# Scaling of the gate one-hots moved from VectorE to ScalarE, eight row requests moved, and a separate buffer for the first gates

## The chip, the cores and the metric

The kernel runs on one core of a Trainium2 chip. The metric is the device time of one execution in microseconds (us). The engines are PE (TensorE, matrix multiply; PEld is its weight load), DVE (VectorE), ACT (ScalarE), POOL (GpSimd) and SP (SyncE, which here only issues DMAs). Each engine works through its own list of instructions in order, and the lists meet only at semaphores.

## The reference, cut to what matters

A two-block network over 512 tokens of width 1024. The change touches the expert layer of the first block. Each token picks 16 of 16,384 experts for each of 8 heads and mixes them with softmax gates:

```python
def peer_ffn(h, wq, sub_keys, u, v):       # D = 1024, 8 heads, top 16
    q = (t @ wq).reshape(PEER_BLOCK, PEER_HEADS, 2, PEER_DQ // 2)
    s = jnp.einsum('tpcd,pckd->tpck', q, sub_keys)
    s1, i1 = lax.top_k(s[:, :, 0], 16); s2, i2 = lax.top_k(s[:, :, 1], 16)
    ...
    top, pos = lax.top_k(cand, 16)         # cand: all s1 + s2; idx = i1 * 128 + i2
    g = jax.nn.softmax(top, axis=-1)
    a = jax.nn.gelu(jnp.einsum('tpkd,td->tpk', u[idx], t), approximate=False)
    return jnp.einsum('tpk,tpkd->td', (g * a), v[idx])
```

## The kernel before, in words

The expert layer is `phase_peer`. It treats the tokens in two ways. For 384 tokens (`DENSE`) it computes all 16,384 experts densely: `gelu(u @ h)` for every expert, times a gate matrix that is zero where an expert wasn't picked, times `v`. For the last 128 tokens it fetches the picked rows of `u` and of `v` from HBM by indirect DMA (`rows_by_index`, issued by POOL, 128 rows of 4 KB a request) and works on them on DVE (`dot`, `row`). Five row buffers (`RING`) are used in turn, so request n waits until row n - 5 was used.

The order of the work is written out by hand in steps g. Steps 0 to 3 are the output projection of the mixer, 4 to 11 the query projection, 12 to 75 the 64 groups of two 128-expert tiles of `u` (steps 12 to 75, "dense steps" below). In a dense step PE does two tiles j = 0, 1 of 24 matmuls each: every fp32 operand is split into a high and a low part (`split3`, lines 997 to 999). The high part `u_high` of step g is made by ACT (`high`, L1300), which may write it only when PE has ended step g - 2. The low part `u_low` is a subtraction, on POOL up to step 43 (L1182) and on DVE from step 44 (`low_u`, L1487). PE waits for it (`u_split`) at the start of the step. ACT also moves each finished tile out of PSUM through Gelu (L1353), into one of four tiles that SP stores (`spill`, L1112).

**Selection, steps 6 to 43.** PE makes scores in 16 units at the steps given by `unit_step` (14, 16, 18, 20, 23, ... 38 for the last twelve), and DVE finds the top 16 of each (`select`). Unit 4 (step 14) is followed by `row_numbers`, which gives the indices for the row requests (`indexed`). From step `PICK_AT` = 16 on, POOL issues the row requests of a step (`pick_step`) and then the subtraction of that step. DVE's products with these rows (`dot`, L1482) come at `dot_step`, ahead of the step's unit. At step 43 PE transposes the selection into `selT`.

**Spread, steps 44 to 67.** The gates are spread to dense form by a matmul of two one-hot matrices for each token. A batch m is 8 tokens, two batches a step: batch 2(g - 44) ahead of tile j = 0 and the next ahead of tile j = 1. DVE builds them (`batch`): one instruction for the eight `one2` (L1496) and eight for `one1`, each compare and multiply by the token's gate (L1499). PE multiplies them (`spread`, L1220), ACT moves the result to `gs` (L1344), and SP stores a block of 32 tokens every two steps.

**Steps 68 to 75** are dense steps with row requests and their products only. After them DVE does the last products, ACT a Gelu over all of them, and the second half begins: 64 groups `down(g)` with `v` (matmuls again at L997 to L999). For each, DVE multiplies the stored Gelu tile by the gates (`weighted`, L1546), ACT makes `v_high` (L1361) and `w_high` (L1365), DVE `v_low` (L1537) and `w_low` (L1553), and then some row sums (`row`, L1530 and L1533). Three of these row sums (`rows_at[0]`) stand between `w_low` of group 0 and the work for group 1; the second of them reads its row into the buffer of `h_tok`, which is free only when all 128 products are done.

Of the kernel before, what the change touches and what calls it, by code (L numbers as in the profile page):

```python
# [16 lines left out]
ALU = mybir.AluOpType  # L17
# [130 lines left out]
def phase_project(k):  # L148
    nc, ps = k.nc, k.ps
    with ExitStack() as ctx:  # L150
# [32 lines left out]
        rows_in, rows = k.sem("c_rows_loaded"), k.sem("c_rows_ready")  # L183
# [100 lines left out]
        def _(dve):  # L284
# [42 lines left out]
            dve.tensor_tensor(c_row[:], c_row[:], row_gate, ALU.mult).then_inc(rows, 1)  # L327
            dve.wait_ge(rows, 1)
# [47 lines left out]
        def _(act):  # L376
# [17 lines left out]
            for j, job in enumerate(jobs):  # L394
                act.wait_ge(proj, j + 1)
                if j == 0:
                    act.wait_ge(rows, 1)
# [604 lines left out]
def phase_peer(k):  # L1002
# [9 lines left out]
    with ExitStack() as ctx:  # L1012
# [36 lines left out]
        w_high, w_low = sb("w_high", [P, 2, GE, DENSE], F32R), sb("w_low", [P, 2, GE, DENSE], F32R)  # L1049

# [4 lines left out]
        gr = [x[:, 0:BLOCKS * 2 * GE * TB].rearrange("p (n j t) -> p n j t", n=BLOCKS, j=2 * GE) for x in u_raw]  # L1055
# [9 lines left out]
        built, mixed, evac, wrote = k.sem("onehots"), k.sem("gates_mm"), k.sem("gates_evac"), k.sem("gates_written", 2)  # L1065
# [41 lines left out]
        def _(sp):  # L1107
# [7 lines left out]
            for g in range(GROUPS):  # L1115
# [18 lines left out]
            def gate_pair(i):  # L1134
                sp.dma_start(gr[i % 2].rearrange("p n j t -> p n (j t)"), gates[i]).then_inc(g_in[i % 2], 16)
# [8 lines left out]

            load(0)
            load(1)
            sp.wait_ge(u_split, WQ_G + U_G)
            gate_pair(0)
# [12 lines left out]
        def _(pool):  # L1161
# [13 lines left out]
            for x in range(WQ_G + U_G):  # L1175
                for n in picks_at[x + OUT_G]:
# [3 lines left out]
                if x + OUT_G < SPREAD_AT:  # L1180
                    pool.wait_ge(u_hi, x + 1)
                    pool.tensor_tensor(u_low[:, x % 2], u_raw[x % 2][:], u_high[:, x % 2].bitcast(F32),  # L1182
                                       ALU.subtract).then_inc(u_split, 1)
# [5 lines left out]
        def _(pe):  # L1189
# [23 lines left out]
            def spread(m):  # L1213
                pe.wait_ge(built, m + 1)
# [79 lines left out]
        def _(act):  # L1294
# [6 lines left out]

            for t in range(KT):
# [10 lines left out]
            for g in range(OUT_G, GROUPS):  # L1313
# [15 lines left out]
                if g == TURN_AT:  # L1329
                    for tt in range(SELF):  # L1330
# [3 lines left out]
                                       ACT.Copy).then_inc(turned_sb, 1)  # L1334
                for j in range(GE):
# [18 lines left out]
                if g + 2 < GROUPS:  # L1354
                    high(g + 2 - OUT_G)

            def high_v(g):
                act.wait_ge(v_in[g % 2], 16 * (g // 2 + 1))
                if g >= 2:
                    act.wait_ge(v_mm, g - 1)  # L1360
                act.activation(v_high[:, g % 2], v_raw[:, g % 2], ACT.Copy).then_inc(v_hi, 1)  # L1361

            def high_w(g):
                act.wait_ge(weighted, g + 1)
                act.activation(w_high[:, g % 2], w[:, g % 2], ACT.Copy).then_inc(w_hi, 1)  # L1365
# [15 lines left out]
        def _(dve):  # L1381
# [108 lines left out]
            def batch(m):  # L1490
# [44 lines left out]
            def low_v(g):  # L1535
                dve.wait_ge(v_hi, g + 1)
# [770 lines left out]
```

## Time and profile before

| what | value |
|---|---|
| median of 3 runs | 2626.16 us (2624.96 to 2630.01) |
| the profiled execution's own time | 2625.34 us |
| its span in the profile | 2623.5 us |
| PE busy | 2431.3 us, 93% |
| DVE busy | 1696.8 us, 65% |
| ACT busy | 879.6 us, 34% |
| POOL busy | 624.4 us, 24% |
| mean granted TensorE clock | 0.958 of full |

The rows further down come from the profiled execution, whose span is 1.8 us shorter than its time and whose time is 0.8 us below the median. A row of the timeline has the start, the duration, the engine and line, the operation with output and inputs, and in brackets the engine's idle time just before, with what ended it. Matmuls overlap: one of 384 columns lasts 0.33 us in the records while the next begins 0.17 us after it.

### The profile page before, as it was taken

How to read it: one execution, taken by the hardware profiler on the slowest of the kernel's cores; microseconds unless marked ns; L12 is line 12 of the kernel's file. 1: busy time of each engine (PE TensorE's matmuls, PEld its weight loads, DVE VectorE, ACT ScalarE, POOL GpSimd, SP SyncE). 2: the span in 40 equal slices, each digit the busy share in tenths (PEclk: the TensorE clock that was granted, in tenths of full speed). 3: DMA queues.
4: the chain of work that ended last, by engine and by line, in shares of the span. 5: the costliest groups of instructions: out<-in, count | busy, mean ns of one | idle time of the engine just before them, and what ended most of it. 6: DMA issues, size and time to landing. Idle time of an engine off the chain costs nothing. (4 is left out here: it accounts for less than half of the span.)

```text
span 2623.5 us, 31224 instructions
## 1 busy us (share of the span) xinstructions
PE 2431.3 (93%) x12267; PEld 2043.3 (78%) x12267; DVE 1696.8 (65%) x3087; ACT 879.6 (34%) x1161; POOL 624.4 (24%) x350
## 2 busy tenths in 40 slices
PE   8899988798898999899999699999999699999997
PEld 7455547674577999899999699999999476667775
DVE  2313438773279798799997678877876635654544
ACT  0200013332223332355554233333332434457333
POOL 0000003230234666633233433333331000000000
PEclk6899999899998999999999899999999899999999
DMA  6446240000223666688899999999995122112122
GB/s 218 168 141 203 97 143 15 1 1 33 100 94 116 213 217 224 192 294 313 321 343 343 352 353 356 353 352 350 355 354 210 53 86 80 49 42 72 56 89 72
DMA packets 180850, 487.07 MB, mean 186 GB/s; under 512 B 13249, under 2 KB 79937, under 8 KB 169185
## 3 DMA queue, kind: packets, MB, share of 16 engines
q1 hardware_dynamic: 143840, 350.85, 39.7%
q0 software_dynamic: 36864, 134.23, 13.4%
q8 instruction: 97, 1.59, 0.2%
q14 instruction: 49, 0.39, 0.0%
HBM read 430.51 MB, written 52.43 MB: 184 GB/s over the span
## 5 line engine op out<-in xcount | busy, mean ns | idle before, releaser
L997 PE MATMUL ps<-h_high,u_high 128*128 128x384 f32 (+1 forms) x1152 | 404.9, 351 | 42.7 <-POOL u_low L1182 33.5
L998 PE MATMUL ps<-h_low,u_high 128*128 128x384 f32 (+1 forms) x1152 | 397.4, 345 | 0.0
L999 PE MATMUL ps<-h_high,u_low 128*128 128x384 f32 (+1 forms) x1152 | 397.2, 345 | 0.0
L997 PE MATMUL ps<-w_high,v_high 128*128 128x384 f32 x1024 | 343.7, 336 | 22.3 <-DVE w_low L1553 22.3
L998 PE MATMUL ps<-w_low,v_high 128*128 128x384 f32 x1024 | 342.9, 335 | 0.0
L999 PE MATMUL ps<-w_high,v_low 128*128 128x384 f32 x1024 | 342.9, 335 | 0.0
L997 PEld LDWEIGHTS ps<-h_high,u_high 128*128 128x128 f32 x1152 | 220.3, 191 | 53.6 <-POOL u_low L1182 36.1
L1361 ACT ACTIVATE v_high<-v_raw 128x2048 fp32r<-128x2048 f32 x64 | 122.6, 1916 | 351.5 <-PE ps L999 351.5
L999 PEld LDWEIGHTS ps<-h_high,u_low 128*128 128x128 f32 x1152 | 220.0, 191 | 5.3
L998 PEld LDWEIGHTS ps<-h_low,u_high 128*128 128x128 f32 x1152 | 220.4, 191 | 4.6
L1537 DVE TENSOR_TENSOR v_low<-v_raw,v_high 128x2048 fp32r<-128x2048 f32 x64 | 146.7, 2292 | 117.7 <-ACT v_high L1361 117.7
L1171 POOL DMA_INDIRECT mixT<-in_peer_v,row_index x102 | 147.9, 1450 | 264.2 <-DVE row_sum L1530 231.8
L997 PEld LDWEIGHTS ps<-w_high,v_high 128*128 128x128 f32 x1024 | 192.9, 188 | 22.6 <-issue 22.6
L1171 POOL DMA_INDIRECT mixT<-in_peer_u,row_index x103 | 148.8, 1444 | 251.1 <-DVE row_dot L1482 216.7
L998 PEld LDWEIGHTS ps<-w_low,v_high 128*128 128x128 f32 x1024 | 193.0, 188 | 0.0
L999 PEld LDWEIGHTS ps<-w_high,v_low 128*128 128x128 f32 x1024 | 192.8, 188 | 0.0
L1353 ACT ACTIVATE gelu<-ps 128x384 f32<-128x384 f32 x128 | 63.5, 497 | 354.8 <-PE ps L999 216.1
L440 PE MATMUL ps<-mixT,ring 128*128 128x512 f32 x384 | 169.6, 600 | 10.9 <-ACT hcT L389 10.9
L2036 DVE TENSOR_TENSOR w_low<-w_raw,w_high 128x1024 fp32r<-128x1024 f32 x70 | 85.7, 1225 | 132.1 <-ACT w_high L1911 132.0
L997 PE MATMUL ps<-h_high,w_high 128*128 128x512 f32 x376 | 152.2, 405 | 13.7 <-DVE h_low L2142 10.4
L440 PEld LDWEIGHTS ps<-mixT,ring 128*128 128x128 f32 x384 | 73.8, 193 | 99.7 <-issue 88.2
L999 PE MATMUL ps<-h_high,w_low 128*128 128x512 f32 x376 | 147.1, 391 | 0.0
(372 smaller groups left out, 4599.3 us busy)
## 6 DMA issues: line engine op xcount, KB each, us to landing
v_raw<-in_peer_v SPq DMA_DIRECT2D x64, 1024.0 KB, 6.3
w_raw<-in_w SPq DMA_DIRECT2D x70, 512.0 KB, 3.5
u_first<-in_uT SPq DMA_DIRECT2D x32, 1024.0 KB, 6.2
u_second<-in_uT SPq DMA_DIRECT2D x32, 1024.0 KB, 6.4
late_w<-in_late_w SPq DMA_DIRECT2D x56, 512.0 KB, 4.2
gelu_up<-gelu SPq DMA_DIRECT2D x128, 192.0 KB, 6.8
gates<-gates_sb SPq DMA_DIRECT2D x12, 2048.0 KB, 12.5
weighted<-gelu_up SPq DMA_DIRECT2D x64, 384.0 KB, 6.6
```

The lines of the kernel that those rows point to most:

```text
L440: last = pe.matmul(ps[:, j % NB, 0:job.N], a, b, start=i == 0, stop=i == KT - 1)
L997: pe.matmul(out, wh, mh, start=start, stop=False)
L998: pe.matmul(out, wh, ml, start=False, stop=False)
L999: return pe.matmul(out, wl, mh, start=False, stop=stop)
L1171: pool.indirect_dma_start(out=row_of(total), out_offset=None, in_=table, in_offset=bass.IndirectOffsetOnAxis(ap=row_no[:, n:n + 1], axis=0))\
L1353: act.activation(gel[:, x % 4, :], ps[:, x % 4, 0:DENSE], ACT.Gelu).then_inc(u_ev, 1)
L1361: act.activation(v_high[:, g % 2], v_raw[:, g % 2], ACT.Copy).then_inc(v_hi, 1)
L1537: dve.tensor_tensor(v_low[:, g % 2], v_raw[:, g % 2], v_high[:, g % 2].bitcast(F32), ALU.subtract)\
L2036: dve.tensor_tensor(wlo[:, i % SPLITS, :], raw[:, i % RAWS, :], whi[:, i % SPLITS, :].bitcast(F32), ALU.subtract).then_inc(w_low, 1)
```

## The change

- `batch` on DVE makes `one1` for the eight tokens with one comparison instruction, without the gates. A new function `scale_ones` on ACT multiplies each of the eight by its gate, in place (8 instructions a batch). It stands at the end of ACT's step g for the batches of step g + 1. PE waits for it (`scaled_one`) and no longer for `built`.
- `pick_step`: 28 row requests in steps 16 to 43, one a step (36 before), 76 in steps 44 to 67 (64 before), 24 in steps 68 to 75 (28 before).
- POOL's subtraction stands ahead of the row requests of its step.
- The first pair of gates is loaded into a buffer of its own (`g_first`), ahead of `load(0)`; in the kernel before it waits for the last `u_split`. The gate blocks are stored one step earlier.
- `weigh`, `low_v`, `low_w` (DVE) and `high_v`, `high_w` (ACT) of group 0 are moved into step 75: on DVE behind `low_u` of step 75 and ahead of its products, on ACT ahead of that step's Gelu.
- The semaphore `rows` is merged into `silu_c`.

```diff
 def pick_step(n):
-    return PICK_AT + 7 * n // 9 if n < 36 else SPREAD_AT + 3 * (n - 36) // 8 if n < 100 else 68 + 2 * (n - 100) // 7
+    return PICK_AT + n if n < 28 else SPREAD_AT + 6 * (n - 28) // 19 if n < 104 else 68 + (n - 104) // 3

 def dot_step(n):
-    return pick_step(n) + (2 if n < 36 else 1)
+    return pick_step(n) + (2 if n < 28 else 1)
...
+        g_first = sb("gates_first", [P, BLOCKS * 2 * GE * TB])
+        def pair_buffer(i):
+            return gr[i % 2 if i else 2]
...
# SyncE
-                while written < BLOCKS and g >= SPREAD_AT + PER_BLOCK * (written + 1) // GE + 4:
+                while written < BLOCKS and g >= SPREAD_AT + PER_BLOCK * (written + 1) // GE + 3:
...
+            gate_pair(0)
             load(0)
             load(1)
             sp.wait_ge(u_split, WQ_G + U_G)
-            gate_pair(0)
             gate_pair(1)
...
# GpSimd
             for x in range(WQ_G + U_G):
+                if x + OUT_G < SPREAD_AT:
+                    pool.wait_ge(u_hi, x + 1)
+                    pool.tensor_tensor(u_low[:, x % 2], u_raw[x % 2][:], u_high[:, x % 2].bitcast(F32),
+                                       ALU.subtract).then_inc(u_split, 1)
                 for n in picks_at[x + OUT_G]:
                     if n == 0:
                         pool.wait_ge(indexed, 1)
                     rows_by_index(n, k.dram["peer_u"], n)
-                if x + OUT_G < SPREAD_AT:
-                    pool.wait_ge(u_hi, x + 1)
-                    pool.tensor_tensor(u_low[:, x % 2], ...).then_inc(u_split, 1)
...
# TensorE
             def spread(m):
-                pe.wait_ge(built, m + 1)
+                pe.wait_ge(scaled_one, m + 1)
...
# ScalarE
+            def scale_ones(m):
+                act.wait_ge(built, m + 1)
+                for j in range(BATCH):
+                    one, t = one1[:, m % 2 * BATCH + j, :], m * BATCH + j
+                    last = act.activation(one, one, ACT.Copy, scale=selT[:, 2, t:t + 1])
+                last.then_inc(scaled_one, 1)
...
             for g in range(OUT_G, GROUPS):
...
+                if g == GROUPS - 1:
+                    high_v(0)
+                    high_w(0)
                 for j in range(GE):
...
                         act.activation(gel[:, x % 4, :], ps[:, x % 4, 0:DENSE], ACT.Gelu).then_inc(u_ev, 1)
                 if g + 2 < GROUPS:
                     high(g + 2 - OUT_G)
+                for j in range(GE):
+                    for m in batches_at(g + 1, j):
+                        scale_ones(m)
...
-            high_v(0)
             act.wait_ge(row_used, PICKS)
             act.activation(row_dot[:], row_dot[:], ACT.Gelu).then_inc(row_gelu, 1)
-            for g in range(U_G):
-                if g:
-                    high_v(g)
+            for g in range(1, U_G):
+                high_v(g)
                 high_w(g)
...
# VectorE, batch(m)
-                for j in range(BATCH):
-                    last = dve.tensor_scalar(one1[:, q + j, :], iota[:], selT[:, 0, t0 + j:t0 + j + 1],
-                                             selT[:, 2, t0 + j:t0 + j + 1], ALU.is_equal, ALU.mult)
-                last.then_inc(built, 1)
+                dve.tensor_tensor(one1[:, q:q + BATCH, :], iota[:].unsqueeze(1).to_broadcast([P, BATCH, P]),
+                                  selT[:, 0, t0:t0 + BATCH].unsqueeze(2).to_broadcast([P, BATCH, P]),
+                                  ALU.is_equal).then_inc(built, 1)
...
             for g in range(OUT_G, GROUPS):
                 if g >= SPREAD_AT:
                     low_u(g - OUT_G)
+                if g == GROUPS - 1:
+                    weigh(0)
+                    low_v(0)
+                    low_w(0)
                 for n in dots_at[g]:
                     dot(n)
...
-            low_v(0)
+            dve.wait_ge(row_gelu, 1)
+            link(dve.tensor_tensor(row_w[:], row_dot[:], row_gate[:], ALU.mult))
             for g in range(U_G):
...
+                if g:
+                    weigh(g)
                     low_v(g)
-                dve.wait_ge(w_hi, g + 1)
-                dve.tensor_tensor(w_low[:, g % 2], ...).then_inc(w_split, 1)
+                    low_w(g)
                 for n in rows_at[g]:
                     row(n)
```

## Rows read from the trace of the kernel before

**Rows 1.** The page: busy time, share of the span, instructions of each engine.
```profile
PE 2431.3 (93%) x12267; PEld 2043.3 (78%) x12267; DVE 1696.8 (65%) x3087; ACT 879.6 (34%) x1161; POOL 624.4 (24%) x350
```

**Rows 2.** PE's own waits, longest first: total us, times, longest.
```profile
PE ps L997 <- POOL u_low L1182: 33.5, 8, 11.8
PE ps L997 <- DVE w_low L1553: 22.3, 1, 22.3
```

**Rows 3.** Stretches: PE, PEld, DVE, ACT, POOL busy, granted clock, DMA share, GB/s.
```profile
1300.00:1400.00 100.00, 99.97 (x671) 99.53 (x670) 97.64 (x206) 58.44 (x61) 34.13 (x24) 1.00 0.88 329
```

**Rows 4.** Timeline of PE and ACT around the end of a spread step.
```profile
1244.32 2.02 PE L1220 MATMUL ps<-one_hots 128*128 128x128 f32 x16
...
1250.37 1.95 PE L1220 MATMUL ps<-one_hots 128*128 128x128 f32 x16
...
1244.47 0.49 ACT L1353 ACTIVATE gelu<-ps 128x384 f32<-128x384 f32 x1 [2.98 <-PE ps L999]
1244.85 1.90 ACT L1300 ACTIVATE u_high<-u_second 128x2048 fp32r<-128x2048 f32 x1
```

**Rows 5.** ACT: timeline and groups of small activations, with and without a scale pointer.
```profile
2614.82 5.01 ACT L2027 ACTIVATE mqkv<-mqkv,cols 128x512 f32<-128x512 f32 x8 [4.15 <-DVE mqkv L2194]
2207.81 0.28 ACT L1960 ACTIVATE at_w<-ps 128x128 f32<-128x128 f32 x1 [2.79 <-DVE ps L2103]
2207.98 0.27 ACT L1961 ACTIVATE at_rest<-ps 128x128 f32<-128x128 f32 x1
...
L1369 ACT ACTIVATE row_dot<-row_dot 128x128 f32<-128x128 f32 x1 | 0.3, 299 | 0.0
L2027 ACT ACTIVATE mqkv<-mqkv,cols 128x512 f32<-128x512 f32 x8 | 5.0, 707 | 4.1 <-DVE mqkv L2194 4.1
```

**Rows 6.** PE timeline: restarts after an idle time, and where the slow matmuls end.
```profile
384.32 3.78 PE L615 MATMUL ps<-ic,ring 128*128 128x128 f32 x16 [4.24 <-ACT ring L749]
846.52 0.69 PE L997 MATMUL ps<-h_high,u_high 128*128 128x384 f32 x1 [11.76 <-POOL u_low L1182]
...
852.13 0.40 PE L999 MATMUL ps<-h_high,u_low 128*128 128x384 f32 x1
914.62 0.44 PE L997 MATMUL ps<-h_high,u_high 128*128 128x384 f32 x1 [2.51 <-POOL u_low L1182]
1087.79 0.69 PE L997 MATMUL ps<-h_high,u_high 128*128 128x384 f32 x1 [8.92 <-POOL u_low L1182]
...
1090.83 0.50 PE L997 MATMUL ps<-h_high,u_high 128*128 128x384 f32 x1
```

**Rows 7.** Groups by shape, DVE and ACT, 1126 to 1400 us: busy, mean ns, idle before.
```profile
L1499 DVE TENSOR_SCALAR one_hots<-iota,selT 128x128 f32<-128x128 f32 x362 | 97.9, 349 | 0.0
L1496 DVE TENSOR_TENSOR one_hots<-iota,selT 128x1024 f32<-128x1024 f32 x45 | 54.7, 1216 | 0.0
...
L1344 ACT ACTIVATE gates_sb<-ps 128x512 f32<-128x512 f32 x92 | 96.3, 1162 | 52.7 <-DMA gates<-gates_sb 47.5 <-PE ps L1220 5.2
```

**Rows 8.** Timeline of POOL in the selection.
```profile
839.53 1.16 POOL L1171 DMA_INDIRECT mixT<-in_peer_u,row_index  x1 [16.17 <-DVE row_index L1476]
...
1081.37 1.69 POOL L1171 DMA_INDIRECT mixT<-in_peer_u,row_index  x1 [9.65 <-DVE row_dot L1482]
```

**Rows 9.** DVE's wait for scores, 835 to 1115 us: total us, times, longest.
```profile
DVE peer_val L1410 <- ACT peer_s L1318: 22.9, 4, 9.8
```

**Rows 10.** Timeline of SP, ACT, DVE and PE behind step 75.
```profile
1481.03 15.33 SPq L1112 DMA_DIRECT2D gelu_up<-gelu  x8
...
1490.74 0.49 ACT L1353 ACTIVATE gelu<-ps 128x384 f32<-128x384 f32 x1 [21.95 <-DMA gelu_up<-gelu]
...
1482.70 1.23 DVE L1482 CUSTOM_DVE_ANT_0 mixT<-mixT,h_by_token 128x1024 f32<-128x1024 f32 x1 [0.30 <-DMA mixT<-in_peer_u,row_index]
...
1503.20 0.66 PE L997 MATMUL ps<-w_high,v_high 128*128 128x384 f32 x1 [22.30 <-DVE w_low L1553]
```

**Rows 11.** DMA issues, 1390 to 1530 us: count, median us to landing.
```profile
mixT<-in_peer_v,row_index POOLq DMA_INDIRECT x10, 7.9
```

More of the change, by code:

```diff
@@ L182, in phase_project @@
         late_in, late_used = k.sem("late_loaded", 2), k.sem("late_used")
-        rows_in, rows = k.sem("c_rows_loaded"), k.sem("c_rows_ready")
+        rows_in = k.sem("c_rows_loaded")
         jobs = []
@@ L326, in _ @@
             dve.wait_ge(sg_c, 2)
-            dve.tensor_tensor(c_row[:], c_row[:], row_gate, ALU.mult).then_inc(rows, 1)
-            dve.wait_ge(rows, 1)
+            dve.tensor_tensor(c_row[:], c_row[:], row_gate, ALU.mult).then_inc(silu_c, 1)
+            dve.wait_ge(silu_c, 3)
             def late_mod(x):
@@ L396, in _ @@
                 if j == 0:
-                    act.wait_ge(rows, 1)
+                    act.wait_ge(silu_c, 3)
                 src = ps[:, j % NB, 0:job.N]
@@ L1064, in phase_peer @@
         spilled = k.sem("gelu_stored", 4)
-        built, mixed, evac, wrote = k.sem("onehots"), k.sem("gates_mm"), k.sem("gates_evac"), k.sem("gates_written", 2)
+        built, scaled_one, mixed, evac, wrote = k.sem("onehots"), k.sem("onehots_scaled"), k.sem("gates_mm"), k.sem("gates_evac"), k.sem("gates_written", 2)
         v_in, v_hi, v_split, v_mm = k.sem("v_loaded", 2), k.sem("v_highs"), k.sem("v_split"), k.sem("v_mm")
@@ L1134, in gate_pair @@
             def gate_pair(i):
-                sp.dma_start(gr[i % 2].rearrange("p n j t -> p n (j t)"), gates[i]).then_inc(g_in[i % 2], 16)
+                sp.dma_start(pair_buffer(i).rearrange("p n j t -> p n (j t)"), gates[i]).then_inc(g_in[i % 2], 16)
             def load(g):
@@ L1300, in high, with high_v, high_w @@
                 act.activation(u_high[:, x % 2], u_raw[x % 2][:], ACT.Copy).then_inc(u_hi, 1)
+            def scale_ones(m):
[4 more added lines that the diff above has]
+                last.then_inc(scaled_one, 1)
+            def high_v(g):
+                act.wait_ge(v_in[g % 2], 16 * (g // 2 + 1))
+                if g >= 2:
+                    act.wait_ge(v_mm, g - 1)
+                act.activation(v_high[:, g % 2], v_raw[:, g % 2], ACT.Copy).then_inc(v_hi, 1)
+            def high_w(g):
+                act.wait_ge(weighted, g + 1)
+                act.activation(w_high[:, g % 2], w[:, g % 2], ACT.Copy).then_inc(w_hi, 1)
             for t in range(KT):
@@ L1497, in batch, with low_v, weigh, low_w @@
                                   selT[:, 1, t0:t0 + BATCH].unsqueeze(2).to_broadcast([P, BATCH, P]), ALU.is_equal)
-                for j in range(BATCH):
-                    last = dve.tensor_scalar(one1[:, q + j, :], iota[:], selT[:, 0, t0 + j:t0 + j + 1],
-                                             selT[:, 2, t0 + j:t0 + j + 1], ALU.is_equal, ALU.mult)
-                last.then_inc(built, 1)
+                dve.tensor_tensor(one1[:, q:q + BATCH, :], iota[:].unsqueeze(1).to_broadcast([P, BATCH, P]),
+                                  selT[:, 0, t0:t0 + BATCH].unsqueeze(2).to_broadcast([P, BATCH, P]),
+                                  ALU.is_equal).then_inc(built, 1)
+            def low_v(g):
+                dve.wait_ge(v_hi, g + 1)
+                dve.tensor_tensor(v_low[:, g % 2], v_raw[:, g % 2], v_high[:, g % 2].bitcast(F32), ALU.subtract)\
+                   .then_inc(v_split, 1)
+            def weigh(g):
+                dve.wait_ge(w_in[g % 2], 16 * (g // 2 + 1))
+                dve.wait_ge(g_in[g // 2 % 2], 16 * (g // 4 + 1))
+                x = w[:, g % 2].rearrange("p j (n t) -> p j n t", t=TB)
+                y = pair_buffer(g // 2)[:, :, g % 2 * GE:(g % 2 + 1) * GE, :].rearrange("p n j t -> p j n t")
+                dve.tensor_tensor(x, x, y, ALU.mult).then_inc(weighted, 1)
+            def low_w(g):
+                dve.wait_ge(w_hi, g + 1)
+                dve.tensor_tensor(w_low[:, g % 2], w[:, g % 2], w_high[:, g % 2].bitcast(F32), ALU.subtract).then_inc(w_split, 1)
             for g in range(OUT_G, GROUPS):
```

27 lines of the change are left out of this document (2 added, 25 removed).

## The prediction

> **What bounds the kernel now.** I read the page's totals first: PE is busy for 93% of the span, every other engine for 65% or less [rows 1]. So time is won or lost where PE stands still. PE's own waits come next: the two long ones are 33.5 us for `u_low` of POOL, in eight pieces of the selection, and one of 22.3 us ahead of `down(0)` [rows 2]. Then the stretches: in the spread (steps 44 to 67, 1124 to about 1414 us) PE is busy all the time at full clock, while DVE stands at 98% and ACT at 58% [rows 3]. No wait of PE lies there. Its own work sets that stage: a batch and a tile take 1250.37 - 1244.32 = 6.05 us [rows 4], a step 12.1 us. DVE is nearly as full, but its relief is worth nothing by itself, since nobody waits for it. What the change puts into PE's path there is what counts.
>
> **Spread, DVE.** A step loses 16 of L1499; they are 362 in 97.9 us of time on the engine, 0.27 each, so 4.3 us. It gains two comparisons of the form of L1496, 1.22 us each [rows 7], and half a product more. DVE falls from 12.1 to about 11 us a step. Price 0: PE was never short of one-hots.
>
> **Spread, ACT: the new wait.** The order on ACT is what decides. At the end of step g it does Gelu of tile j = 1, which waits for PE's last matmul of the step; then `high(g + 2)`, which also needs PE to be through step g; and only then `scale_ones` of both batches of step g + 1. PE begins step g + 1 with the first of these batches. Queued behind PE's new wait are that batch and all 48 matmuls of the step, and nothing of step g is left to PE. So once a step PE stands still for the whole chain, however early DVE built the one-hots. The terms: Gelu starts at 1244.47, `u_high` 0.38 us later and lasts 1.90 [rows 4], of which 1.80 pass before a successor can start. For the eight scalings the nearest row is the in-place copy with a scale pointer, L2027: 0.707 us for 512 columns, eight in 5.01, so 0.62 from start to start [rows 5]. A column costs 0.83 ns: 1.90 us for 2048 columns [rows 4] less 0.299 for 128 (L1369 [rows 5]), over 1920. So 384 columns fewer take 0.32 off: 0.39 us long, 0.30 apart. Eight are 7 x 0.30 + 0.39 = 2.5 us. With 0.1 us to hand over, the gap is 0.38 + 1.80 + 2.5 + 0.1 = 4.8 us. Below: activations of 128 columns without a pointer follow each other in 0.17 us [rows 5], so eight take 1.45 and the gap is 3.7. Above: no overlap at all, 8 x 0.39 = 3.1, gap 5.4. I take 4.8, the row with a pointer being the same form.
>
> The row of 128 columns without pointers says 0.299 us [rows 5]. The Trainium skill (ScalarE: Activation LUTs, section "What ACT_TABLE_LOAD costs") prices an activation at 186 ns + 0.833 ns a column, 93 ns more for each pointer operand, and lets neighbours overlap by 93 ns; it agrees with that row (293 ns), and by it eight scalings would take 7 x 0.293 + 0.386 = 2.4 us, an estimate that would make the gap 4.7 us and the stage 2 us cheaper than the sum here.
>
> The second batch isn't late: it's scaled 2.4 us after the first, and PE has 6 us of work until then. ACT's step, 58% of 12.1 us plus 16 x 0.30 = 4.8 us, is 11.9 us and fits into the longer step. How often: the batches of steps 44 to 67 each stand behind such a chain, 24 gaps, 24 x 4.8 = 115 us.
>
> **Spread, clock.** After each long gap PE restarts slowly. Behind 4.24 us of idleness 16 matmuls of 128 columns took 3.78 us [rows 6] where they take 2.02 in the spread [rows 4]. The low level (1.2 of 2.4 GHz) lasted from 846.52 to 852.13 and from 1087.79 to 1090.83 [rows 6], 5.6 and 3.0 us, about half of it lost; behind 2.51 us of idleness the matmuls ran at full speed at once (0.44 us). A gap of 4.8 us is on the side of those that cost. I take 4.1 us at the low level, 1.9 lost (ends 1.4 and 2.6; nothing, if the clock stays up): 24 x 1.9 = 46 us. Stage: +161 us.
>
> **Spread, ACT's wait for the store.** The gates now leave a step earlier, which takes away ACT's 47.5 us of waits on them [rows 7]. Price 0: PE never waited for it, and ACT has time in the longer step. If the store still came late, up to 5.9 us would be added to a gap every two steps; SP reaches it a full step (12 us) earlier, so I take nothing.
>
> **Selection.** POOL's request waits for DVE's product (9.65 us), the subtraction is queued behind it, and PE behind that; likewise the first request waits 16.17 us for the indices, the subtraction of step 16 behind it, and PE stands for 11.76 us until 846.52 [rows 6, 8]. With the subtraction first and one request a step, subtraction g needs only the products of step g - 4 (before: of about g - 2), while DVE, which spends about 20 us on a unit with its products (240 us for eleven, below), is behind PE by some 2.3 steps at most when it starts each unit on time. So the eight waits go. One is left: the request at 839.5 now holds the subtraction of step 17, ready at 839.5 + 1.2 + 4.6 = 845.3, while PE, which could start step 16 at 846.52 - 11.76 = 834.8, wants it one step (8.4 us of matmuls and 0.6 of scores) later, at 843.8: 1.5 us. Saved: 33.5 [rows 2] + about 6 of slow restarts (2.6 + 1.4 from [rows 6], two short ones) - 1.5 = 38 us. What is late next: DVE's own chain. The request that it releases at 1081.37 [rows 8] is for the first product behind the last of eleven units, which began when the indices were there, at 839.3. Of these 241 us it stood 22.9 [rows 9], in waits that a PE on time mostly takes away, and eight products of 1.2 us leave the stage: the selection would end near 1055, 25 us earlier, against 38 for PE. PE used it at 1114, over 30 us behind the last unit, of which the exponential, the softmax and the products between take some 10. So about 10 us are left, and it doesn't bind. Ends: 25 (DVE and stores bind in part) and 42. The requests moved to the spread add 12 products of 1.2 us to DVE there, hidden by its free time.
>
> **Step 75 and the first groups.** Before, SP's stores of Gelu tiles were issued at 1481.03, behind the gate pairs, and ACT stood 21.95 us for them; PE got group 0 at 1503.20 [rows 10], 22.7 us after step 75 (1480.5). With the first pair out of the way I expect the stores 8 us earlier (half of the 18 us that both pairs and the first store took), so Gelu of step 74 ends some 3 us after step 75. `high_v`, `low_v` and `low_w` take 1.9, 2.3 and 1.0: `w_low(0)` is ready 8 us after step 75, and `down(0)` starts. But now the products of steps 75 and 76 stand behind `low_w(0)` on DVE. From there: product 1.2, request 1.7, landing 7.9 [rows 11], product 1.2, requests of the `v` rows 3.2 (the second needs all products), landing 7, row 1.3, then `weigh`, `low_v`, `low_w` of group 1 with 4.1: 27.6 us. `down(1)` starts 36 us after step 75. Before: 22.7 + 8.4 = 31.1, as all products were done at 1483.9 [rows 10]. +5, and 2.3 for a second slow restart: +7. Ends: +11, and -8 if the rows land fast or the stores leave earlier. So the visible wait goes and a new one takes its place behind `down(0)`.
>
> **Merged semaphore**: the same wait on the same instruction; 0.
>
> **Sum.** 161 - 38 + 7 = +130 us. On the profiled execution's 2625.3 that is 2755.3; the median is 0.8 higher, so 2756.
>
> **The rivals.**
> 1. The clock stays up through gaps of 4 to 5 us. For it: the row at 2.51 us; against: the row at 4.24 us [rows 6]. 115 - 38 + 7 = +84: 2710.
> 2. The selection gives nothing back, because DVE's units (then `selected`, at step 43) or the stores of Gelu tiles hold PE where POOL did. For it: DVE stands for only 22.9 of 241 us [rows 9]. Against: the slack of about 10 us worked out above. +161 + 7 = +168: 2794.
> 3. Scaling on the SBUF operand is dearer (0.39 us, no overlap): 24 x 0.6 = 15 us more, 2771.
> 4. The other side: the scaling is hidden. It needs the scaled batch to be ready before PE ends its step. For it: DVE has built it by then, and ACT is idle for 42% [rows 3]. Against: it stands behind the Gelu of PE's last tile in ACT's list. If hidden, -38 + 7 = -31: 2595. It decides for faster once the gap with its restart is below 31 / 24 = 1.3 us; the cheapest chain is 3.7.
> 5. The change doesn't do what it says: the gaps are there, but only as long as the gain, no change. That needs the same 1.3 us.
>
> **How the numbers follow.** Forecast 0.60, its own range 2725 to 2785 (3.7 and 5.4 us gaps: -26 and +15; the ends of the other terms). Rival 1: 0.14; rival 2: 0.10; rival 3: 0.07; rival 4: 0.06; rival 5 and its like: 0.03. The range 2705 to 2790 takes in the forecast, rivals 1 and 3, and leaves out 2, 4 and 5: about 0.19. A measurement of this kernel can tell some 0.2% (5 us) from no change. Faster 0.07, within 0.2% 0.02, slower 0.91.
>
> **What the profile would show.** Right: PE waits 24 times at L1220 for ACT's scaling, 4.5 to 5 us each, 115 us in all; the steps 44 to 67 are 18 to 19 us long; the granted clock of that stretch is well below 1.00; 384 scalings of 0.39 us; the waits at L997 for POOL's `u_low` are one or two; DVE in the spread is below 65%; no wait ahead of `down(0)` over 10 us and one of 10 to 20 us ahead of `down(1)`. Wrong: if PE waits for nothing in the spread (rival 4), if its matmuls are fast right after each gap (rival 1), or if waits for `u_low` or `selected` stay near 30 us (rival 2).

## The result and the profile after

| | before | after |
|---|---|---|
| median, both timed in one series on the same chip | 2625.56 us (2624.47 to 2630.01) | 2760.06 us (2758.13 to 2761.38) |
| span of the profiled execution | 2623.5 us | 2759.6 us |
| mean granted TensorE clock | 0.958 | 0.942 |

The ratio is 1.0516, with a 95% interval of 1.0503 to 1.0528: the changed kernel is 5.2% slower. The forecast was 2756 us.

The page of the kernel after, busy time of each engine (against [rows 1]):

```profile
PE 2480.7 (90%) x12267; PEld 2086.7 (76%) x12267; DVE 1674.6 (61%) x2751; ACT 995.9 (36%) x1545; POOL 615.9 (22%) x350
```

PE has the same instructions and is busy 49 us longer, so they ran at a lower clock; the rest of the 136 us of span is idle. PE's own waits of the kernel after show where (total us, times, longest):

```profile
PE ps L1227 <- DVE u_low L1505: 109.4, 23, 4.8
PE ps L997 <- DVE w_low L1534: 17.2, 2, 10.6
PE ps L997 <- POOL u_low L1185: 10.6, 5, 6.0
PE ps L1227 <- ACT one_hots L1313: 4.8, 1, 4.8
PE ps L1259 <- DVE peer_sel L1555: 3.5, 1, 3.5
```

L1227 is the spread matmul: 24 waits, 114.2 us, that were not there before. The waits for `u_low` fell from 33.5 to 10.6 us [rows 2]. The releaser that the first line names can't be right: the `u_low` that ends there is made from the `u_high` of step g + 2, and PE wants it only a step later. The timeline of the kernel after, of PE, ACT and DVE around one such wait:

```profile
1194.99 0.34 PE L999 MATMUL ps<-h_high,u_low 128*128 128x384 f32 x1
1200.09 3.40 PE L1227 MATMUL ps<-one_hots 128*128 128x128 f32 x16 [4.76 <-DVE u_low L1505]
...
1195.37 0.49 ACT L1380 ACTIVATE gelu<-ps 128x384 f32<-128x384 f32 x1 [3.03 <-PE ps L999]
1195.76 1.90 ACT L1307 ACTIVATE u_high<-u_first 128x2048 fp32r<-128x2048 f32 x1
1197.56 4.77 ACT L1313 ACTIVATE one_hots<-one_hots,selT 128x128 f32<-128x128 f32 x16
...
1197.69 2.29 DVE L1505 TENSOR_TENSOR u_low<-u_first,u_high 128x2048 fp32r<-128x2048 f32 x1 [4.13 <-ACT u_high L1307]
```

It is the chain of the forecast, in its order: PE's last matmul, Gelu, `u_high` 0.39 us later, the scalings 1.80 later. Of 16 scalings, the first eight end at 1197.56 + 7 x 0.29 + 0.39 = 1199.98, and PE starts 0.1 us later. `u_low`, which here waits only for the same `u_high`, also ends at 1197.69 + 2.29 = 1199.98; that is how its name came into the list. An experiment below pulls the two ends apart. The 16 matmuls then take 3.40 us in place of 2.02 [rows 4].

Stretches (columns as in [rows 3]) and ACT's groups by shape, 1126 to 1500 us, kernel after:

```profile
1200.00:1500.00 300.00, 224.35 (x1280) 219.71 (x1280) 170.14 (x182) 185.27 (x367) 67.95 (x51) 0.86 0.62 223
```

```profile
L1313 ACT ACTIVATE one_hots<-one_hots,selT 128x128 f32<-128x128 f32 x314 | 93.8, 388 | 0.0
L1371 ACT ACTIVATE gates_sb<-ps 128x512 f32<-128x512 f32 x80 | 85.1, 1110 | 16.0 <-PE ps L1227 16.0
```

In the spread PE is busy 75% of the time at a clock of 0.86, where it was busy all the time at 1.00 [rows 3]; DVE stands at 57%, ACT at 62%. No engine is full: the stage is a chain. ACT's 47.5 us of waits for the stored gates [rows 7] are gone and nobody gained by it.

**Where the 136 us come from.** Up to 625 us, ahead of the changed part, the trace after is already 2.4 us late; the runs below differ there by up to 5 us in the same code. Step 44 starts at 1100.1 (before: 1123.7), 26 us earlier if those 2.4 are taken off. From there to the end of step 75 it is 518.0 us (before: 357.2), +160.8: 114.2 of gaps and 46.6 of slow matmuls, 1.94 a step. From there to the start of `down(1)`, 1618.1 to 1646.1, it is 28.0 us; before, 1480.9 to 1513.6, it was 32.7. Behind it 3.6 us are lost: 1.9 in the slow matmuls of `down(1)`, the rest behind the last group, in code that the change leaves alone. 2.4 - 26 + 160.8 - 4.7 + 3.6 = 136.

### The profile page after: what moved, and what is told of

It reads as the page before. It is cut to its first block and busy times, and to the rows that moved or that the text cites. A ratio compares the mean times of both kernels' runs of the same rounds, so it can differ in the third digit from the quotient of the medians.

```text
span 2759.6 us, 31272 instructions
## 1 busy us (share of the span) xinstructions
PE 2480.7 (90%) x12267; PEld 2086.7 (76%) x12267; DVE 1674.6 (61%) x2751; ACT 995.9 (36%) x1545; POOL 615.9 (22%) x350
## 5 line engine op out<-in xcount | busy, mean ns | idle before, releaser
L997 PE MATMUL ps<-h_high,u_high 128*128 128x384 f32 (+1 forms) x1152 | 407.0, 353 | 18.6 <-POOL u_low L1185 10.6
L1227 PE MATMUL ps<-one_hots 128*128 128x128 f32 x768 | 132.4, 345 | 114.2 <-DVE u_low L1505 109.4
L1227 PEld LDWEIGHTS ps<-one_hots 128*128 128x128 f32 x768 | 126.8, 256 | 121.2 <-DVE u_low L1505 121.2
L1178 POOL DMA_INDIRECT mixT<-in_peer_u,row_index x103 | 135.9, 1319 | 364.7 <-DVE row_dot L1500 335.1
L997 PEld LDWEIGHTS ps<-w_high,v_high 128*128 128x128 f32 x1024 | 193.8, 189 | 17.8 <-DVE v_low L1522 10.9
L440 PE MATMUL ps<-mixT,ring 128*128 128x512 f32 x384 | 169.1, 599 | 10.9 <-ACT hcT L389 10.9
## 6 DMA issues: line engine op xcount, KB each, us to landing
gates<-gates_sb SPq DMA_DIRECT2D x12, 2048.0 KB, 12.7
```

The lines of the kernel that those rows point to most:

```text
L440: last = pe.matmul(ps[:, j % NB, 0:job.N], a, b, start=i == 0, stop=i == KT - 1)
L997: pe.matmul(out, wh, mh, start=start, stop=False)
L1178: pool.indirect_dma_start(out=row_of(total), out_offset=None, in_=table, in_offset=bass.IndirectOffsetOnAxis(ap=row_no[:, n:n + 1], axis=0))\
L1227: last = pe.matmul(ps[:, bank, i * P:(i + 1) * P], one2[:, j, :], one1[:, j, :], start=True, stop=True)
```

## The experiments

All ratios are against the kernel before, run on the same chip in the same series (medians of it 2624.5 to 2625.1 us).

### The two halves

`x1_only_scaling`: the kernel before, with the scaling edit (comparison without gates, `scale_ones` at the end of ACT's step, PE waits for `scaled_one`) and the merged semaphore. `x2_rest_alone`: the kernel after without it:

```diff
-                pe.wait_ge(scaled_one, m + 1)
+                pe.wait_ge(built, m + 1)
...
-                for j in range(GE):
-                    for m in batches_at(g + 1, j):
-                        scale_ones(m)
```

> The kernel before with the scaling on ScalarE alone (at the end of ScalarE's step, as in the change), everything else as before. Theory A (the scalings stand behind Gelu and u_high of the step's end, so PE stands 4.76 us a step and restarts slowly; the rest of the change gives time back): +161 us, 2787. Rival B (the slowdown comes from the parts together, e.g. from the row requests moved into the spread): clearly less, below 2760.

> The changed kernel with the scaling put back into VectorE's one-hot instruction; all other parts of the change stay. Theory A: 2760 - 161 = 2599, with no wait of PE in the spread. Rival B: above 2620. It also prices the rest of the change: the traces say some 26 us from the selection and about 0 from the step 75 part.

Measured: x1 2788.25 us, ratio 1.0623 (1.0606 to 1.0641), +163.8; x2 2604.54 us, 0.993 (0.9914 to 0.9947), -20. Added to the kernel before, or to x2 (2760 - 2604.5), the scaling costs 164 or 155.5 us. The two differ because x2 loses 8 us of its own from step 44 to 75 (365.2 us against 357.2). PE's waits of x2:

```profile
PE ps L997 <- DVE w_low L1525: 17.9, 2, 11.2
PE ps L997 <- POOL u_low L1185: 10.6, 5, 6.0
PE ps L1227 <- issue: 7.8, 7, 1.9
```

The spread has small new waits, 7.8 us, that the kernel before had not: with 12 more products in it DVE is full (window of x2), and PE does stand for its one-hots now and then. The requests alone do this: x6 below has 8.0 us in six such waits, x5 and x7 have 2.3 and 2.5 in three.

```profile
1200.00:1380.00 180.00, 176.10 (x1169) 173.20 (x1168) 178.88 (x372) 100.45 (x103) 66.22 (x45) 1.00 0.88 334
```

### Is the order on ACT the cause?

`x4_scale_before_high`: the scalings ahead of `u_high` (the rival to be told apart: the gap is `u_low`'s, as the list of waits says). `x3_scale_early`: the first batch's scalings inside the step, ahead of the wait for tile j = 1.

```diff
# x4, against the kernel after
-                if g + 2 < GROUPS:
-                    high(g + 2 - OUT_G)
                 for j in range(GE):
                     for m in batches_at(g + 1, j):
                         scale_ones(m)
+                if g + 2 < GROUPS:
+                    high(g + 2 - OUT_G)
# x3, against the kernel after
+                    if j == 1:
+                        for m in batches_at(g + 1, 0):
+                            scale_ones(m)
                     act.wait_ge(u_mm, x + 1)
...
-                for j in range(GE):
-                    for m in batches_at(g + 1, j):
-                        scale_ones(m)
+                for m in batches_at(g + 1, 1):
+                    scale_ones(m)
```

> The changed kernel with the scalings of a step placed ahead of u_high but still behind the step's last Gelu. Theory A: u_high (1.80 us) leaves the chain, the gap falls from 4.76 to 2.96 us, 24 x 1.8 = 43 us less, 2717; less still if the clock stays up through some of the shorter gaps (down to 2675). Rival D (PE is released by VectorE's u_low, as the trace's list of waits has it, which now comes later): no gain, 2760 or more.

> The changed kernel with all 384 scalings still on ScalarE, but the first batch of step g + 1 scaled ahead of the Gelu of tile j = 1 of step g, the second behind u_high. Theory A (only the place counts): the gaps vanish, 2600. Rival C (ScalarE has too much work with 4.8 us of scaling in a 12 us step, wherever it stands): ScalarE sets the pace, 2640 to 2760.

x4: 2703.73 us, 1.0304 (1.0287 to 1.0321), 56 less than after. Timeline of x4, ACT and PE:

```profile
1196.63 0.49 ACT L1380 ACTIVATE gelu<-ps 128x384 f32<-128x384 f32 x1 [2.99 <-PE ps L999]
1197.02 4.77 ACT L1313 ACTIVATE one_hots<-one_hots,selT 128x128 f32<-128x128 f32 x16
1201.69 1.90 ACT L1307 ACTIVATE u_high<-u_second 128x2048 fp32r<-128x2048 f32 x1
...
1199.55 2.92 PE L1227 MATMUL ps<-one_hots 128*128 128x128 f32 x16 [2.95 <-issue]
1216.27 2.61 PE L1227 MATMUL ps<-one_hots 128*128 128x128 f32 x16 [2.96 <-issue]
1232.97 2.02 PE L1227 MATMUL ps<-one_hots 128*128 128x128 f32 x16 [2.95 <-issue]
1248.09 3.62 PE L1227 MATMUL ps<-one_hots 128*128 128x128 f32 x16 [2.96 <-issue]
```

PE starts at 1199.55, before `u_high` even begins and so before the `u_low` that follows it: `u_low` is not what it waits for. Each gap is 4.76 - 2.95 = 1.8 us shorter, which is the pass time of `u_high`; 24 of them make 43 us, and the other 13 come from the clock. After gaps of one length the restart is fast (2.02 us) in 4 of the 24 steps and takes 2.5 to 3.65 us in the others, some 0.3 less from one step to the next until it is fast once.

x3: 2622.57 us, 0.9994 (0.9984 to 1.0003): no difference from before, 18 us slower than x2, and neither the 2600 of theory A nor the 2640 of rival C. The long gaps are gone (PE's waits at L1227: 19.7 us in 22, longest 3.3), but the step doesn't fall back to 12.1 us: it takes 12.7 us in 14 of the 20 steps from 47 on, and 13.0 to 13.8 in the rest. Timeline of x3, ACT, DVE and PE:

```profile
1242.01 2.45 ACT L1313 ACTIVATE one_hots<-one_hots,selT 128x128 f32<-128x128 f32 x8 [0.95 <-DVE one_hots L1518]
1244.73 1.90 ACT L1307 ACTIVATE u_high<-u_first 128x2048 fp32r<-128x2048 f32 x1
...
1246.66 2.29 DVE L1507 TENSOR_TENSOR u_low<-u_first,u_high 128x2048 fp32r<-128x2048 f32 x1 [2.42 <-ACT u_high L1307]
...
1244.56 2.02 PE L1227 MATMUL ps<-one_hots 128*128 128x128 f32 x16 [0.52 <-issue]
```

DVE waits 2.42 us for ACT's `u_high`; then come `u_low`, the products and the one-hots, for which ACT waits 0.95 us before it scales; and only behind the scalings comes the next `u_high`. Scaling 2.36, Gelu 0.36, `u_high` 1.9, `u_low` 2.2, three products 3.45, two comparisons 2.3 add up to 12.6 us: a ring over two engines, as long as the step, with neither of them full (ACT 88%, DVE 81% of 1200 to 1380 us). The ring is read from the trace; no run took it apart.

### What the rest of the change is made of

One part each, in the kernel before: `x5_order_only` (POOL's subtraction ahead of the requests), `x6_picks_only` (`pick_step` and `dot_step`), `x7_group0_only` (`g_first`, `gate_pair(0)` ahead of `load(0)`, group 0 in step 75; the diff of that part stands under the change).

```diff
# x5, POOL
-                for n in picks_at[x + OUT_G]:
-                    ...
                 if x + OUT_G < SPREAD_AT:
                     ...
+                for n in picks_at[x + OUT_G]:
+                    ...
# x6
-    return PICK_AT + 7 * n // 9 if n < 36 else SPREAD_AT + 3 * (n - 36) // 8 if n < 100 else 68 + 2 * (n - 100) // 7
+    return PICK_AT + n if n < 28 else SPREAD_AT + 6 * (n - 28) // 19 if n < 104 else 68 + (n - 104) // 3
```

> The kernel before with one edit: GpSimd's subtraction ahead of the row requests of its step (36 requests in the selection as before). Theory E (the wait for row_dot is what held the subtraction): most of the 33.5 us of waits for u_low go; 2624 - 20 to - 26, 2600, if the order is the part that counts. If the number of requests counts, no more than - 8 here.

> The kernel before with one edit: 28 row requests in the selection in place of 36, one a step, and the rest spread over the later steps. A request of a step still stands ahead of its subtraction. If one request a step is enough to free the subtraction: - 10 to - 20 us; the wait of 11.8 us for the indices at step 16 must stay, since the first request still stands ahead of the subtraction of step 16.

> The kernel before with the own buffer for the first gates and the work of group 0 moved into step 75, nothing else of weight (the merged semaphore is in it). The prediction said + 7 us, the trace of the changed kernel (two waits of 6.6 and 10.6 us and two slow restarts in place of one wait of 22.3) says 0 to - 3: 2622 to 2631.

| | us | ratio (95%) | PE's waits for POOL's `u_low` |
|---|---|---|---|
| x5 | 2617.42 | 0.997 (0.9958 to 0.9982) | 26.6 in 9, longest 8.9 |
| x6 | 2605.53 | 0.9932 (0.992 to 0.9945) | 17.9 in 8, longest 10.5 |
| x7 | 2628.96 | 1.0018 (1.001 to 1.0027) | 33.6 in 8, longest 11.8 |

-7.3, -19.2 and +4.3 add up to -22, against -20 for the three together (x2, which also has the earlier gate stores): they act almost separately. Fewer requests do most, part of it behind step 75, where the wait for `w_low` falls from 22.3 to 18.6 us. x5 misses the 2600 that its expectation set for the order: a wait of 7.3 us at step 17 takes the place of the one of step 16, and one of 8.9 stays at 1087 us, behind a request that stood 9.66 us for DVE's product. x7 is a small loss, where its expectation had 0 to - 3 in a range up to 2631; its two waits for `w_low` (23.6 us, longest 12.7) replace the one of 22.3 [rows 2].

### Why the selection gave 26 us and not 38

Of PE's waits, 1.5 us were to be left. Measured are five for `u_low`, 10.6 us, and 3.5 for the selection: 12.6 more, which is all of the 12 us. DVE's idle time did vanish (waits for scores 22.9 us [rows 9], now 1.4), yet DVE was hardly sooner: its last unit ended at 1077.6, before at 1079.4. Timeline of DVE and POOL, kernel after:

```profile
831.13 4.00 DVE L1441 CAST peer_indf<-peer_ind 128x64 f32<-128x64 uint32 x1
...
830.46 4.62 POOL L1185 TENSOR_TENSOR u_low<-u_first,u_high 128x2048 fp32r<-128x2048 f32 x1 [4.61 <-ACT u_high L1307]
...
952.04 4.37 DVE L1461 TENSOR_SCALAR peer_half<-peer_pos 128x32 uint32<-128x32 uint32 x1
956.33 0.17 DVE L1462 TENSOR_SCALAR peer_half<-peer_pos 128x32 uint32<-128x32 uint32 x1
...
951.76 4.62 POOL L1185 TENSOR_TENSOR u_low<-u_second,u_high 128x2048 fp32r<-128x2048 f32 x1 [3.12 <-ACT u_high L1307]
...
1032.83 1.23 DVE L1500 CUSTOM_DVE_ANT_0 mixT<-mixT,h_by_token 128x1024 f32<-128x1024 f32 x1
1033.98 5.63 DVE L1500 CUSTOM_DVE_ANT_0 mixT<-mixT,h_by_token 128x1024 f32<-128x1024 f32 x1
...
1033.29 5.24 POOL L1185 TENSOR_TENSOR u_low<-u_first,u_high 128x2048 fp32r<-128x2048 f32 x1 [3.50 <-ACT u_high L1307]
...
1083.61 4.17 DVE L1555 TENSOR_TENSOR peer_sel<-peer_sel,peer_small 128x384 f32<-128x384 f32 x1
...
1082.82 4.54 POOL L1185 TENSOR_TENSOR u_low<-u_second,u_high 128x2048 fp32r<-128x2048 f32 x1 [1.51 <-ACT u_high L1307]
```

An instruction of 0.18 us takes 4.37 and ends 0.03 us after POOL's subtraction (956.38 against 956.41); a product of 1.2 us takes 5.63 and ends 1.08 us after one (1038.53 against 1039.61), as if it had begun there. The product at 1032.83 began ahead of the subtraction and kept its 1.23; there the subtraction took 5.24 instead of 4.62. From the indices to the end of the last unit, conversions, integer operations and products last 21.9 us longer than their shortest in 17 instructions in the kernel before (26.3 in 18 with one comparison of 5.11 us), and 46.7 us in 22 after. So DVE lost in standing instructions what it gained in waits: the eleven units took 232 us, with 21.5 us less of waits and six products fewer than in the 240 us before.

Two of these instructions lie where PE feels them. The conversion of unit 4 (4.00 us, 0.19 before) makes the indices 3.8 us late: with the subtraction first, POOL subtracts just then, where before it stood in the request. x5, which has that order alone, shows the same delay, and x6, which hasn't, doesn't. And L1555 is the last product of the softmax, for which PE stood 3.5 us; in x8 below it takes 0.90.

The Trainium skill (SBUF — State Buffer, section "SBUF: two separate sides") says that DVE and GpSimd share one port pair as an exclusive lock: a DVE instruction with two SBUF inputs, or in a mode that uses both ports, and a GpSimd instruction that reads SBUF shut each other out, and the one that starts first has the pair until it ends. The trace agrees, with 956.38 against 956.41 above; which mode the conversions ran in, no run shows.

`x8_subtraction_in_four` (x2 with POOL's subtraction as four instructions of 512 columns) asks whether shorter holds free DVE.

```diff
-                    pool.tensor_tensor(u_low[:, x % 2], u_raw[x % 2][:], ..., ALU.subtract).then_inc(u_split, 1)
+                    for q in range(4):
+                        part = slice(q * KT * GW2 // 4, (q + 1) * KT * GW2 // 4)
+                        last = pool.tensor_tensor(u_low[:, x % 2, part], u_raw[x % 2][:, part], ..., ALU.subtract)
+                    last.then_inc(u_split, 1)
```

> The changed kernel with the scaling back on VectorE (2604.5 us) and GpSimd's subtraction issued as four instructions of 512 columns in place of one of 2048. Theory F (VectorE's CAST, integer TENSOR_SCALAR and product instructions stand still until a running GpSimd subtraction has ended, 46.8 us in the selection): no such instruction lasts longer than some 1.5 us over its usual time, the sum falls below 20 us, the selection is ready some 10 us earlier or more, PE's wait of 3.5 us for it goes, the indices come 3 us earlier; 2604.5 - 5 to - 12. Rival G (they are slowed by DMA traffic or by memory bandwidth in general): the long instructions stay as long, no gain.

2602.1 us, 0.9912 (0.9898 to 0.9927). The excess of the same three kinds falls to 27.7 us, and the longest product takes 2.31 us in place of 5.63. But other instructions now stand that hadn't: 19 additions, comparisons and multiplications of 512 columns (L1437, L1457 and L1462, usually 0.68 us) take 1.7 to 1.8, 20.0 us more. Together it is 47.7 us in 51 instructions, no less than the 46.7 in 22 of x2, and the eleven units take 232 us in both (DVE, then POOL, timeline of x8):

```profile
1028.82 2.30 DVE L1493 CUSTOM_DVE_ANT_0 mixT<-mixT,h_by_token 128x1024 f32<-128x1024 f32 x1
...
1001.20 3.37 DVE L1457 TENSOR_TENSOR peer_pick<-peer_half,io 128x512 f32<-128x512 uint32 x2
...
999.76 5.96 POOL L1187 TENSOR_TENSOR u_low<-u_second,u_high 128x512 fp32r<-128x512 f32 x4 [3.37 <-ACT u_high L1310]
```

Cutting the subtraction spreads the standing over more instructions and doesn't lessen it. Four pieces take up to 6.0 us, not 4.6, since now POOL stands too. What x8 gains lies outside the units: the indices come 6.6 us earlier than in x2 (838.3 against 844.9; 1.6 of it is there already at 620 us), and the softmax product takes 3.3 us less; PE's transposes of the selection come 10 us earlier. PE's waits for `u_low` and the selection fall from 14.1 to 9.8 us (9 of them for `u_low`, longest 3.4), and the time by 2.4 us, less than can be told. The expectation of - 5 to - 12 was missed. That the instructions stand behind each other is shown, and rival G is out, since the long ones end with the pieces. That the missing 12 us are owed to it is supported by the two instructions above, not shown by a time.

### Behind step 75, and a version that beats both

`x9_group0_products_first` is x2 with the last products ahead of group 0, and with three stores of Gelu tiles ahead of SP's wait and `gate_pair(1)`:

```diff
+                for n in dots_at[g]:
+                    dot(n)
                 if g == GROUPS - 1:
+                    for n in dots_at[GROUPS]:
+                        dot(n)
                     weigh(0)
...
+            for g in range(GROUPS - 4, GROUPS - 1):
+                spill(g)
             sp.wait_ge(u_split, WQ_G + U_G)
             gate_pair(1)
```

`x10_second_batch_on_act` is x9 with the gates multiplied by ACT for every second batch only, the one that PE wants 6 us after the step's start. `x11_requests_later` is x10 with each row request of the selection a step later. `x12_subtraction_in_two` is x11 with the subtraction in two pieces.

```diff
# x10, ACT, behind high(g + 2)
+                for m in batches_at(g + 1, 1):
+                    scale_ones(m)
# x11, POOL
-                for n in picks_at[x + OUT_G]:
+                for n in [n for s in ([step - 1] if step < SPREAD_AT else ...) for n in picks_at[s]]:
```

> The changed kernel with the scaling back on VectorE (2604.5 us), and two changes of order: VectorE does the last two steps' products ahead of the work of group 0, and SyncE issues the Gelu stores of steps 72 to 74 ahead of the second gate pair. Theory H (the wait of 10.6 us ahead of down(1) is the chain from w_low(0) through six products and two landings, the wait of 6.6 us ahead of down(0) is the stores behind the gate pair): both waits and their slow restarts (2.3 us each) go, 17.8 + 4.6 = 22 us less, 2582. If the row sums ahead of group 1 wait for something else (DMA traffic), the wait ahead of down(1) stays and the gain is below 12.

> The kernel of the run above with ScalarE scaling only the second batch of a step, which PE needs 6 us after the step's start; the first batch is scaled on VectorE again. Theory A (a scaling costs PE nothing where PE has work until it's done): no gap at the first batch. VectorE loses 1 us of work a step, so the short waits of the spread (7.8 us in seven) go too: 5 to 8 us below the run above. Rival C (ScalarE has no room for it): 10 us or more above it.

> The kernel of the run above with GpSimd's row requests of the selection issued one step later, so that the request that waits for the indices stands behind the subtraction of step 17. Theory E: the wait of 6.0 us and its slow restart (2.5 us) go, 8 us less; part of it comes back as a longer wait for the selection (3.5 us now), if VectorE's chain binds: then 3 to 5 less.

> The kernel of the run above with GpSimd's subtraction as two instructions of 1024 columns. Theory F (VectorE stands until a running GpSimd subtraction ends): the selection is ready some 5 us earlier, and if the wait for it binds, 2 to 5 us less. If the subtractions, which then stand for VectorE in their turn, are what PE waits for, no gain.

| | us | ratio (95%) |
|---|---|---|
| x9 | 2593.06 | 0.9888 (0.9871 to 0.9905) |
| x10 | 2592.43 | 0.9882 (0.9864 to 0.99) |
| x11 | 2589.43 | 0.9867 (0.9851 to 0.9884) |
| x12 | 2599.31 | 0.9899 (0.9882 to 0.9915) |

x9 gains 11.5 us on x2, half of what was expected: the wait ahead of `down(1)` (11.2 us) has gone. The run has two edits, but the stores moved nothing that PE waits for (the wait ahead of `down(0)` stays at 6.6 us), so it was the products behind `w_low(0)` that made it. Timeline of x9, SP and ACT:

```profile
1443.91 0.43 SPq L1147 DMA_DIRECT2D v_raw<-in_peer_v  x1
1444.39 1.08 SPq L1150 DMA_DIRECT2D weighted<-gelu_up  x1
1445.52 18.35 SPq L1119 DMA_DIRECT2D gelu_up<-gelu  x6
...
1462.55 0.96 ACT L1374 ACTIVATE gelu<-ps 128x384 f32<-128x384 f32 x2 [14.69 <-DMA gelu_up<-gelu]
```

ACT waits for a store although SP began to issue them at 1445.5. Ahead of them in the same queue are the loads of `v` and of the stored tiles, issued just before; that these hold the stores up is argued from the order of the rows and wasn't tried.

x10 moves the time by less than can be told. That the scaling of the second batch on ACT makes no gap was confirmed (PE waits 6.8 us in 9 at the spread matmul, 7.0 in 7 in x9), and that DVE, busy for 93% of 1200 to 1380 us in place of 99% in x2, would free PE of the short waits was not. x11 took the wait of step 17 away, and most of it came back as a longer wait for the selection:

```profile
PE ps L1265 <- DVE peer_sel L1568: 10.7, 1, 10.7
PE ps L997 <- DVE w_low L1545: 7.3, 1, 7.3
PE ps L997 <- POOL u_low L1186: 5.7, 6, 1.5
PE ps L1233 <- issue: 5.2, 7, 1.6
```

So with POOL out of the way DVE's own chain sets the end of the selection. x12 lost 9.9 us on x11. With the instructions of 512 columns its excess on DVE was 51.2 us in 33, against 46.3 in 24, so again two pieces lessened nothing; its wait for the selection was 6.9, but a new wait of 4.5 us for one-hots and one more for `w_low` came up. Some 5.7 of the 12 us between the two traces lie in code that the edit leaves alone. Why is not settled. x11 has the lowest median: 2589.4 us, 1.3% faster than before, 6.2% faster than the change as made; x9 and x10 are too near for an order.

## Why the prediction was right

**Spread, +161: measured +160.8.** Each term held: 24 waits, 4.76 us each (predicted 4.8), made of 0.39, 1.80, 2.4 and 0.1; 1.94 us a step for the clock (1.9); steps of 18.3 and 19.3 us (18 to 19). 314 scalings last 388 ns each, and 16 take 4.77 us, so they start (4.77 - 0.39) / 15 = 0.292 us apart. The predicted 0.30 came from a row of another width; the price of the Trainium skill (ScalarE: Activation LUTs, "What ACT_TABLE_LOAD costs") gave 386 and 293 ns, which this trace confirms. x4 shows that ACT's order sets the gap, x1 that the scaling makes the loss.

**Selection, -38: measured -26, mis-sized.** What failed are the sentences "So the eight waits go. One is left" and "So about 10 us are left, and it doesn't bind". Five waits for `u_low` were left, where the signs had one or two. The indices came at 845.5, or 843.1 without the 2.4 us, and not at 839.3, and PE's wait at step 17 was 6.0 us and not 1.5. The two next longest (1.5 and 2.3 us) stand behind requests that waited 5.63 us each for DVE's product, so DVE was further behind PE than the prediction had it. The last unit ended at 1077.6 and not near 1055, and PE stood 3.5 us for the selection; later requests (x11) turned that into 10.7. The working took DVE's instructions at their usual length, and the new order and a denser DVE make them meet POOL's subtractions more often. The lower end, 25 us ("DVE and stores bind in part"), was the place of the result.

**Step 75, +7: measured about -1 in the trace (28.0 - 32.7 + 3.6), +4.3 alone (x7), mis-sized.** The new wait came as described, 10.6 us ahead of `down(1)`. In x7 the two waits are longer, 10.9 and 12.7 us against 6.6 and 10.6, with the row requests and gate stores as in the kernel before; which of these does it was not tried. DVE and POOL, kernel after:

```profile
1623.53 0.95 DVE L1534 TENSOR_TENSOR w_low<-weighted,w_high 128x768 fp32r<-128x768 f32 x1
1632.38 1.23 DVE L1500 CUSTOM_DVE_ANT_0 mixT<-mixT,h_by_token 128x1024 f32<-128x1024 f32 x1 [2.18 <-DMA mixT<-in_peer_u,row_index]
1638.38 1.28 DVE L1567 SCALAR_TENSOR_TENSOR row_sum<-h_by_token,row_weight,row_sum 128x1024 f32<-128x1024 f32 x1 [3.30 <-DMA h_by_token<-in_peer_v,row_index]
1645.04 0.95 DVE L1534 TENSOR_TENSOR w_low<-weighted,w_high 128x768 fp32r<-128x768 f32 x1
...
1625.89 1.69 POOL L1178 DMA_INDIRECT mixT<-in_peer_u,row_index  x1 [21.95 <-DVE row_dot L1500]
1633.89 1.31 POOL L1178 DMA_INDIRECT h_by_token<-in_peer_v,row_index  x1 [4.02 <-DVE row_dot L1500]
```

```profile
1624.74 0.66 PE L997 MATMUL ps<-w_high,v_high 128*128 128x384 f32 x1 [6.61 <-DVE w_low L1534]
1646.14 0.66 PE L997 MATMUL ps<-w_high,v_high 128*128 128x384 f32 x1 [10.56 <-DVE w_low L1534]
```

From `w_low(0)` to `w_low(1)` it is 21.5 us, not 27.6: the last product starts 6.8 us after the one that frees its buffer (1625.6 to 1632.4), where 1.7 + 7.9 had been taken, and the last awaited row sum (1640.8) 7.2 us after that product's end, where 3.2 + 7 had been. The rows landed sooner than the median of [rows 11]. So the step that failed is the term of 27.6 us. The 31.1 us of the prediction for the kernel before left out the slow restart that lies in the 32.7.

**Terms of nothing.** DVE's relief in the spread, the earlier gate stores and the merged semaphore: no wait of PE appears or goes with them, though no run had the earlier stores or the semaphore alone. The 12 products more were costed at nothing, hidden by DVE's free time; that cover exists only while ACT does the scaling. In x2 it is gone, and PE stands 7.8 us.

**Rivals.** The clock didn't stay up (rival 1): 3.40 us for 16 matmuls, 0.86 granted. The selection gave back 26 us (rival 2). The scaling wasn't dearer (rival 3). Nothing was hidden in the kernel after (rivals 4 and 5); x3 took most of the gap away and then ended level with before, which the price of 1.3 us a gap didn't foresee: the ring through ACT and DVE takes over. In all, +161 - 26 - 1 = +134, against +130 predicted: two errors, +12 and -8, partly cancel. The mechanism and its largest term were right; that the time came within 4 us is in part luck.

## What to carry to other kernels

Before work moves to an idle engine, look at where it lands in that engine's list: here a 2.4 us job stood behind the Gelu that ends the consumer's own step, on an engine idle for 42% of the time, and cost 6.7 us a step. If the producer must stay there, give it what is wanted later (in x10 that cost nothing, and gained nothing that can be told) or put it ahead of the wait, and then check for a ring through the engine that feeds it (x3). An engine's slack worked out from usual durations is too large where a neighbour can make its instructions stand. And before shorter pieces are called a cure, add up all instructions that stand, not only those that stood before: x8 looked like 47 us falling to 28, and was 47 to 48.

## What of the hardware was not expected

- DVE's conversions, integer operations and products stand until GpSimd's subtraction ends: up to 4.00 us (conversion), 4.37 (32 integers) and 5.63 (product), 46.7 us of 232 in the kernel after. Not all stand: in the kernel before DVE's index searches kept their 0.28 us while POOL subtracted from 841.97 to 846.47, and only the conversion that began at 844.48 stood until 846.53.
- Gaps of one length don't cost the same: after 2.95 us 16 matmuls took between 2.02 and 3.65 us (x4, granted clock 0.91 from 1200 to 1500 us), where one gap of 2.51 us had cost nothing [rows 6]. A gap of 4.76 us costs 1.94 us on top of itself.
- Two requests for indirect rows behind step 75 had their rows in use 4.5 and 6.5 us after they started (1633.9 to 1638.4, 1625.9 to 1632.4), where the median to landing before was 7.9 [rows 11].
